# Prompt attention: the order in which ScalarE moves turned probabilities and takes exponentials

## The chip, the cores and the metric

The kernel runs on one core of a Trainium2 chip. The metric is the device time of one execution in microseconds (us). Before the change three runs took 2003.85, 2005.93 and 2006.01 us, with a median of 2005.93 us. Durations below come from one more execution, taken with the hardware profiler.

Five engines work side by side, each through its own instruction list in order: TensorE (PE; its weight loads are the rows "PEld"), VectorE (DVE), ScalarE (ACT), GpSimd (POOL) and SyncE (SP). They meet only at semaphores.

## The reference, cut to what matters

The program is one inference step of a decoder layer for a prompt of 512 tokens and 8 sample sequences of 8 tokens. The change touches only the prompt's sparse attention. There 8 query heads share 2 key/value heads, and each query attends in three branches, each with its own softmax: 31 compressed keys, selected blocks, and a sliding window. With 512 prompt tokens the selected blocks and the window both come to every earlier key.

```python
scale = NSA_HD ** -0.5
s_c = jnp.einsum('qhgd,nhd->qhgn', q, kc) * scale
p_c = masked_softmax(s_c, m_c, -1)
o_c = jnp.einsum('qhgn,nhd->qhgd', p_c, vc.astype(jnp.float32))
...
s_s = jnp.einsum('qhgd,qhnld->qhgnl', q, k_sel) * scale
p_s = masked_softmax(s_s, m_s, (-2, -1))
o_s = jnp.einsum('qhgnl,qhnld->qhgd', p_s, v_sel.astype(jnp.float32))
s_w = jnp.einsum('qhgd,khd->qhgk', q, win_k) * scale
p_w = masked_softmax(s_w, m_w, -1)
o_w = jnp.einsum('qhgk,khd->qhgd', p_w, win_v.astype(jnp.float32))
return gates[..., 0:1] * o_c + gates[..., 1:2] * o_s + gates[..., 2:3] * o_w
```

The softmax is exp(s - max) divided by its sum; the kernel takes the maximum on VectorE, the exponential with its sum on ScalarE, and the division as a factor on the output.

## The kernel before

The program is a row of stages (`project`, `gla`, `compress`, `prompt_attention`, `sample_attention`, `output_and_router`, `experts`, `combine`). All engines meet in a barrier after each stage, so a stage starts when the slowest engine has ended the one before it.

`prompt_attention` (L1053) works through 16 units, u = 0 to 15. A unit is one tile of 128 queries (tile t = u // 4) and one head of each of the two key/value groups (g = u % 4). It uses (t+1) x 128 keys, so that units 0 to 3 have 128 keys, 4 to 7 have 256, 8 to 11 have 384, and 12 to 15 have 512. For each unit:

- TensorE computes the scores: `score_cmp(u)` (L1267, L1268) for the compressed keys, `scores(u, 0)` and `scores(u, 1)` (L1279, L1284) for the selected and the window branch.
- VectorE takes the maxima: `max_cmp(u)` (L1201) and `maxima(u, b)` (L1209), each ended by the small operation of `negated` (L1194).
- ScalarE takes the exponentials: `exp_cmp(u)` (two instructions, L1143) and `exps(u, b)` (two instructions, L1152). In the profile each has a companion row that reads the accumulator.
- TensorE turns the probabilities so that keys lie on partitions: `to_key_major(u, r)` (L1295 for r = 0, L1300 for r = 1 to 4). Here r = 0 is the compressed branch, 1 and 2 are the selected branch's two heads, 3 and 4 the window's. The results go alternately to two PSUM banks, so turn number k waits until turn number k-2 has been moved out.
- ScalarE moves r = 0, 2, 4 out of PSUM and VectorE moves r = 1, 3 (`move`, L1135 on ScalarE, L1111 on VectorE).
- TensorE multiplies by the values, `values(u)` (L1312, L1320), ScalarE copies that result out (`copy_out(u)`, also a row of L1135, 128x384), TensorE turns it back, `back(u)` (L1331), and VectorE weighs and adds (`finish(u)`, first row L1227).

The order of each engine is written out by hand. TensorE's loop body for unit u is: `scores(u+1, 0)`, turns 0 and 1, `score_cmp(u+1)`, turns 2, 3 and 4, `scores(u+1, 1)`, `back(u-1)`, `values(u)`. VectorE's is: `maxima(u, 1)`, `maxima(u+1, 0)`, move 1, `max_cmp(u+1)`, move 3, `finish(u-1)`, `factors(u)`. `back(u-1)` writes to the bank that holds the compressed scores of unit u+1, and so it waits for `exp_cmp(u+1)`:

```python
pe.wait_ge(s_oc, u + 1)
pe.wait_ge(s_pc, min(u + 3, NU))
```

(here u is the unit turned back.)

Of the kernel before, what the change touches and what calls it, by code (L numbers as in the profile page):

```python
# [1052 lines left out]
def prompt_attention(core):  # L1053
# [34 lines left out]
    s_pt, s_pta, s_ptd = (core.sem(n) for n in ("pT_ps", "pT_by_act", "pT_by_dve"))  # L1088
# [3 lines left out]
    def keys_of(u):  # L1092
        return (u // GRP + 1) * P
# [10 lines left out]
    def move(eng, u, r, copy):  # L1104

        k = NR * u + r
        eng.wait_ge(s_pt, k + 1)
        if r == 0:
            return copy(pTc[0:NCMP_P], ps[0:NCMP_P, TURN + k % 2, 0:KVH * P].rearrange("p (h n) -> p h n", h=KVH))
        b, h = divmod(r - 1, KVH)  # L1110
        return copy(pT[:, b, h, 0:keys_of(u)], ps[:, TURN + k % 2, 0:keys_of(u)])  # L1111

    with nc.Block() as block:
        @block.gpsimd
        def _(pool):
            for h in range(KVH):
                rows = slice(64 * (1 - h), 64 * (1 - h) + 64)
                pool.memset(kzc[rows, h * NCMP_P:(h + 1) * NCMP_P], 0.0).then_inc(s_zero, 1)
            pool.wait_ge(core.s_table, 16)
            for b in range(1, HELD, 2):  # L1120
                load_past(core, pool, b, past_numbers(core, pool, b))
# [10 lines left out]
        @block.scalar  # L1132
        def _(act):
            def copy(o, s):
                return act.activation(o, s, ACT.Copy)  # L1135

            act.activation(gates[:, 0:ST, :], proj[:, 0:ST, C_NG:C_NG + 24], ACT.Exp, scale=-1.0)
            act.activation(gates[0:64, ST, :], proj[0:64, ST, C_NG:C_NG + 24], ACT.Exp, scale=-1.0).then_inc(s_ge, 1)

            def exp_cmp(u):  # L1140
                act.wait_ge(s_mc, u + 1)
                for h in range(KVH):
                    last = act.activation(pc[:, u % 2, h, :], ps[:, BACK, CMP + h * NCMP_P:CMP + (h + 1) * NCMP_P], ACT.Exp,  # L1143
                                          scale=SC, bias=mx[:, u % 2, h:h + 1], accum_out=su[:, u % 2, h:h + 1])
                last.then_inc(s_pc, 1)

            def exps(u, b):
                nk = keys_of(u)
                act.wait_ge(s_m[b], u + 1)
                for h in range(KVH):  # L1150
                    i = 2 + 2 * b + h
                    last = act.activation(pp[:, u % 2, b, h, 0:nk], ps[:, 2 * b + h, 0:nk], ACT.Exp, scale=SC,  # L1152
                                          bias=mx[:, u % 2, i:i + 1], accum_out=su[:, u % 2, i:i + 1])
                last.then_inc(s_p[b], 1)

            def copy_out(u):
                act.wait_ge(s_o, u + 1)
                copy(oT, ps[:, OUT, 0:3 * P].rearrange("p (b n) -> p b n", b=3)).then_inc(s_oc, 1)

            exp_cmp(0)  # L1160
            exps(0, 0)
            for u in range(NU):
                exps(u, 1)
                if u >= 1:
                    copy_out(u - 1)
                move(act, u, 0, copy).then_inc(s_pta, 1)
                if u + 1 < NU:
                    exps(u + 1, 0)
                    exp_cmp(u + 1)
                for r in (2, 4):  # L1170
                    move(act, u, r, copy).then_inc(s_pta, 1)
            copy_out(NU - 1)

        @block.vector
# [1506 lines left out]
```

## Time and profile before

| | |
|---|---|
| median of three runs | 2005.93 us |
| the profiled execution's own time | 2008.63 us |
| its span (first to last instruction) | 2006.9 us |
| prompt attention in the span | about 415 to 572 us |
| TensorE / VectorE / ScalarE busy over the span | 88% / 73% / 55% |
| mean granted clock of TensorE over the span | 0.92 of full speed |

A row of the profile's timeline gives the start, the duration, the engine, the source line, the operation, output and input, the count of instructions merged in the row, and in brackets how long the engine stood idle before it and which instruction released it. The share of busy time is a mean over stages that differ; the stage of the change is read by itself.

### The profile page before, as it was taken

To read this page: it belongs to the slowest core of one execution; us is meant where nothing else is said; L and a number is where in the kernel's file an instruction comes from. 1 tells how busy PE (TensorE), PEld (TensorE's weight loads), DVE (VectorE), ACT (ScalarE), POOL (GpSimd) and SP (SyncE) were. 2 spreads that over 40 slices of the span, in tenths; PEclk is the share of its full clock that TensorE was granted. 3 is DMA by queue.
4 is the path that set the end of the run, shared out by engine and by line. 5 is a ranking of instruction groups with operands and counts; after the bars stand their busy time and mean duration, and the time that the engine had idled before them with its cause. 6 is when DMAs were issued, how large, how long until landed. Compare 5 with 4: busy or idle time off the path is not lost. (4 is left out here: it accounts for less than half of the span.)

```text
span 2006.9 us, 27108 instructions
## 1 busy us (share of the span) xinstructions
PE 1774.5 (88%) x8969; PEld 1374.5 (68%) x8969; DVE 1458.5 (73%) x1372; ACT 1103.6 (55%) x1040; POOL 284.4 (14%) x311
## 2 busy tenths in 40 slices
PE   4999757877867795899999999999999999999982
PEld 3777645655545443688888888888888888888872
DVE  4421267344544266889999999999999999999993
ACT  3211233334423131667777777777777777777772
POOL 0000100230001040111212112121211212112110
PEclk9999877967878896899999999999999999999996
DMA  9353351450002713789999999999999999999973
GB/s 357 117 188 121 71 163 47 125 189 1 1 1 65 250 60 148 272 317 371 368 376 365 371 366 369 375 365 375 367 370 374 366 374 373 372 370 363 382 273 115
DMA packets 112070, 516.53 MB, mean 257 GB/s; under 512 B 25853, under 2 KB 47117, under 8 KB 59242
## 3 DMA queue, kind: packets, MB, share of 16 engines
q1 hardware_dynamic: 99098, 485.77, 64.7%
q0 software_dynamic: 12912, 29.98, 5.5%
q8 instruction: 35, 0.57, 0.1%
q14 instruction: 25, 0.20, 0.0%
HBM read 502.69 MB, written 31.81 MB: 266 GB/s over the span
## 5 line engine op out<-in xcount | busy, mean ns | idle before, releaser
L2349 PE MATMUL banks<-split 128*128 128x512 f32 x4608 | 1082.0, 394 | 1.6 <-DVE split L2504 1.6
L2349 PEld LDWEIGHTS banks<-split 128*128 128x128 f32 x4608 | 863.6, 189 | 195.7 <-issue 14.7
L2504 DVE TENSOR_TENSOR split<-expert_buffers,split 128x2048 fp32r<-128x2048 f32 x384 | 867.6, 2286 | 63.1 <-ACT split L2439 61.1
L2439 ACT ACTIVATE split<-expert_buffers 128x2048 fp32r<-128x2048 f32 x384 | 733.3, 1917 | 251.5 <-PE banks L2349 232.7
L2287 POOL TENSOR_TENSOR expert_buffers<-routing 128x1 f32<-128x1 f32 x63 | 61.1, 970 | 912.5 <-PE banks L2356 530.9
L443 PE MATMUL banks<-w_in_high,hT_high 128*128 128x476 f32 (+1 forms) x240 | 93.4, 389 | 7.7 <-DVE hT_low L369 7.7
L443 PE MATMUL banks<-w_in_low,hT_high 128*128 128x476 f32 (+1 forms) x240 | 91.7, 382 | 0.0
L382 DVE COPY arena<-banks 128x476 f32<-128x476 f32 (+1 forms) x15 | 9.8, 651 | 112.3 <-PE banks L443 112.3
L443 PE MATMUL banks<-w_in_high,hT_low 128*128 128x476 f32 (+1 forms) x240 | 91.4, 381 | 0.0
L302 ACT ACTIVATE arena<-banks 128x476 f32<-128x476 f32 (+1 forms) x15 | 8.5, 567 | 126.5 <-PE banks L443 126.5
L2508 DVE TENSOR_TENSOR split<-banks,split 128x1024 fp32r<-128x1024 f32 x64 | 77.8, 1215 | 0.2 <-ACT split L2442 0.2
L1887 PE MATMUL banks<-arena 128*128 128x512 f32 (+1 forms) x160 | 74.3, 624 | 0.6 <-ACT arena L1955 0.6
L1152 ACT ACTIVATE arena<-banks,arena 128x128 f32<-128x128 f32 (+3 forms) x64 | 32.9, 517 | 68.1 <-DVE arena L1194 68.1
L2442 ACT ACTIVATE split<-banks 128x1024 fp32r<-128x1024 f32 x64 | 64.7, 1010 | 9.6 <-PE banks L2356 9.6
L443 PEld LDWEIGHTS banks<-w_in_high,hT_high 128*128 128x128 f32 (+1 forms) x240 | 43.2, 180 | 30.3 <-issue 21.5
L2462 ACT ACTIVATE expert_buffers<-banks,expert_buffers 128x1024 f32<-128x1024 f32 x32 | 35.7, 1117 | 46.3 <-PE banks L2349 46.3
L1300 PE MATMUL banks<-arena 128*128 128x128 f32 x160 | 33.0, 325 | 28.3 <-ACT arena L1135 27.3
L1887 PEld LDWEIGHTS banks<-arena 128*128 128x128 f32 (+1 forms) x160 | 29.7, 189 | 40.3 <-issue 39.5
L2310 POOL DMA_INDIRECT ffn_rows<-expert_buffers x32 | 53.0, 1656 | 5.3 <-issue 5.3
L443 PEld LDWEIGHTS banks<-w_in_high,hT_low 128*128 128x128 f32 (+1 forms) x240 | 43.2, 180 | 9.5
L443 PEld LDWEIGHTS banks<-w_in_low,hT_high 128*128 128x128 f32 (+1 forms) x240 | 43.2, 180 | 8.7
L2454 ACT ACTIVATE expert_buffers<-expert_buffers 128x1024 f32<-128x1024 f32 x32 | 34.0, 1062 | 26.1 <-DVE expert_buffers L2515 26.1
(336 smaller groups left out, 1810.6 us busy)
## 6 DMA issues: line engine op xcount, KB each, us to landing
expert_buffers<-in_w_gate SPq DMA_DIRECT2D x128, 1024.0 KB, 7.6
expert_buffers<-in_w_up SPq DMA_DIRECT2D x128, 1024.0 KB, 7.4
expert_buffers<-in_w_down SPq DMA_DIRECT2D x128, 1024.0 KB, 8.8
arena<-in_w_ada SPq DMA_DIRECT2D x16, 1024.0 KB, 4.8
w_in_landing<-in_w_in SPq DMA_DIRECT2D x6, 1904.0 KB, 15.9
arena<-in_w_ada SPq DMA_DIRECT2D x4, 2048.0 KB, 19.2
arena<-in_x_prompt SPq DMA_DIRECT2D x8, 512.0 KB, 10.1
arena<-in_cache_cmp POOLq DMA_DIRECT2D x32, 128.0 KB, 3.5
```

The lines of the kernel that those rows point to most:

```text
L443: last = pe.matmul(ps[0:n, 4 + (NT * c + t) % 4, 0:CW], h[:, kt, t0:t0 + n].bitcast(F32R), w[:, kt, :].bitcast(F32R), start=(kt == 0 and j ...
L1300: last = pe.transpose(ps[:, TURN + k % 2, kb * P:(kb + 1) * P], pp[:, u % 2, b, h, kb * P:(kb + 1) * P], ident)
L1887: last = pe.matmul(ps[0:n, 4 + 2 * (t % 2) + c, :], mixT[:, kt, t0:t0 + n], wout[:, kt, c * 512:(c + 1) * 512], start=(kt == 0), stop=(kt ...
L2287: pool.tensor_tensor(sums[s_sum.index(sem)], one, one, ALU.add).then_inc(sem, 1)
L2310: pool.indirect_dma_start(core.ffn_d, bass.IndirectOffsetOnAxis(ap=row_out.bitcast(U32), axis=0), y, None, bounds_check=NTOK - 1, oob_is_e ...
L2349: last = pe.matmul(ps[:, bank + c, :], x[:, kt * P:(kt + 1) * P].bitcast(F32R), wt.bitcast(F32R), start=False, stop=(kt == KT - 1 and x is ...
L2439: act.activation(high[:, j % RING_Q].bitcast(F32R), v, ACT.Copy).then_inc(s_high, 1)
L2442: act.activation(dst.bitcast(F32R), ps[:, TB:TB + 2, :].rearrange("p b n -> p (b n)"), ACT.Copy).then_inc(sem, 1)
L2454: act.activation(s, g, ACT.Sigmoid, scale=ALPHA).then_inc(s_sig, 1)
L2462: act.activation(y, ps[:, DB:DB + 2, :].rearrange("p b n -> p (b n)"), ACT.Copy, scale=weight_out).then_inc(s_y, 1)
L2504: dve.tensor_tensor(rest[:, j % RING_Q].bitcast(F32R), v, high[:, j % RING_Q], ALU.subtract).then_inc(s_rest, 1)
L2508: dve.tensor_tensor(lo.bitcast(F32R), ps[:, TB:TB + 2, :].rearrange("p b n -> p (b n)"), hi, ALU.subtract).then_inc(out, 1)
```

## The change

In ScalarE's loop the exponentials of the next unit's selected and compressed branch, which stood between move 0 and move 2 of a unit, are issued after move 4, the compressed one first. The window exponentials are only written at another place of the loop: they still follow and still precede the next unit's `copy_out`.

```diff
             exp_cmp(0)
             exps(0, 0)
+            exps(0, 1)
             for u in range(NU):
-                exps(u, 1)
                 if u >= 1:
                     copy_out(u - 1)
-                move(act, u, 0, copy).then_inc(s_pta, 1)
+                for r in (0, 2, 4):
+                    move(act, u, r, copy).then_inc(s_pta, 1)
                 if u + 1 < NU:
+                    exp_cmp(u + 1)
                     exps(u + 1, 0)
-                    exp_cmp(u + 1)
-                for r in (2, 4):
-                    move(act, u, r, copy).then_inc(s_pta, 1)
+                    exps(u + 1, 1)
             copy_out(NU - 1)
```

The instructions on every other engine keep their order. On ScalarE, in units 13 and 14 (512 keys), these rows stand before the change; L1152 are exponentials, L1143 the compressed exponentials, L1135 with 128x384 is `copy_out`, with 31x256 move 0, with 128x512 moves 2 and 4:

```order
L1152 ACTIVATE arena<-banks,arena 128x512 x2
L1135 ACTIVATE arena<-banks 128x384
L1135 ACTIVATE arena<-banks 31x256
L1152 ACTIVATE arena<-banks,arena 128x512 x2
L1143 ACTIVATE arena<-banks,arena 128x31 x2
L1135 ACTIVATE arena<-banks 128x512 x2
L1152 ACTIVATE arena<-banks,arena 128x512 x2
L1135 ACTIVATE arena<-banks 128x384
L1135 ACTIVATE arena<-banks 31x256
```

and these stand there after it:

```order
L1152 ACTIVATE arena<-banks,arena 128x512 x4
L1135 ACTIVATE arena<-banks 128x384
L1135 ACTIVATE arena<-banks 31x256
L1135 ACTIVATE arena<-banks 128x512 x2
L1143 ACTIVATE arena<-banks,arena 128x31 x2
L1152 ACTIVATE arena<-banks,arena 128x512 x4
L1135 ACTIVATE arena<-banks 128x384
```

Between move 0 and move 2 four exponentials have gone; they now stand behind move 4, where the window's two follow them directly.

On ScalarE at the start of the stage (units 0 and 1, 128 keys) the difference is:

```order
 L1152 ACTIVATE arena<-banks,arena 128x128 x4
 L1135 ACTIVATE arena<-banks 31x256
-L1152 ACTIVATE arena<-banks,arena 128x128 x2
-L1143 ACTIVATE arena<-banks,arena 128x31 x2
 L1135 ACTIVATE arena<-banks 128x128 x2
-L1152 ACTIVATE arena<-banks,arena 128x128 x2
-L1135 ACTIVATE arena<-banks 128x384
-L1135 ACTIVATE arena<-banks 31x256
-L1152 ACTIVATE arena<-banks,arena 128x128 x2
-L1143 ACTIVATE arena<-banks,arena 128x31 x2
+L1143 ACTIVATE arena<-banks,arena 128x31 x2
+L1152 ACTIVATE arena<-banks,arena 128x128 x4
```

The four exponentials of unit 0 alone before the loop are the same; from move 0 on the same exchange is made in each of the units 0 to 14.

## Rows read from the trace of the kernel before

**Rows 1.** The page's head.
```profile
span 2006.9 us, 27108 instructions
```

**Rows 2.** Stretches, TensorE alone: length, PE busy (instructions), granted clock, DMA share, GB/s.
```profile
core 0: us, PE busy (x), PEclk, DMA share, GB/s
415.00:450.00 35.00, 30.56 (x185) 0.50 0.83 271
450.00:571.00 121.00, 95.63 (x744) 0.81 0.00 1
573.00:650.00 77.00, 56.74 (x436) 0.82 0.14 43
```

**Rows 3.** Waits from 415 to 572 us: total us, times, longest.
```profile
ACT arena L1152 <- DVE arena L1194: 68.1, 20, 5.9
DVE arena L1227 <- PE banks L1331: 49.1, 16, 4.7
PE banks L1300 <- ACT arena L1135: 27.3, 25, 2.5
```

**Rows 4.** Timeline of unit 14 (512 keys), from turn 2 to `back`.
```profile
552.32 1.09 PE L1300 MATMUL banks<-arena 128*128 128x128 f32 x8 [1.10 <-ACT arena L1135]
...
553.50 0.26 ACT L1143 ACTIVATE arena<-banks,arena 128x31 f32<-128x31 f32 x1
...
553.93 0.19 ACT L1143 ACTIVATION_READ_ACCUMULATOR arena<-banks,arena 128x1 f32 x1
554.02 0.57 ACT L1135 ACTIVATE arena<-banks 128x512 f32<-128x512 f32 x1
...
554.65 0.65 PE L1300 MATMUL banks<-arena 128*128 128x128 f32 x4 [1.24 <-ACT arena L1135]
...
555.34 0.60 ACT L1135 ACTIVATE arena<-banks 128x512 f32<-128x512 f32 x1 [0.74 <-PE banks L1300]
...
556.40 0.55 PE L1331 MATMUL banks<-arena 128*128 128x128 f32 x3
```

**Rows 5.** Timeline of unit 15, the last: turns 2 and 3, turn 4's weights.
```profile
562.45 2.46 PE L1300 MATMUL banks<-arena 128*128 128x128 f32 x12 [2.47 <-ACT arena L1135]
...
563.79 0.71 PEld L1300 LDWEIGHTS banks<-arena 128*128 128x128 f32 x4 [0.44 <-ACT arena L1135]
```

**Rows 6.** Timeline of unit 2 (128 keys), from turn 2 to `back`.
```profile
434.77 0.69 PE L1300 MATMUL banks<-arena 128*128 128x128 f32 x2 [0.35 <-ACT arena L1135]
...
435.83 0.25 ACT L1135 ACTIVATE arena<-banks 128x128 f32<-128x128 f32 x1
436.13 0.48 PE L1300 MATMUL banks<-arena 128*128 128x128 f32 x1 [0.68 <-ACT arena L1135]
...
436.65 0.28 ACT L1135 ACTIVATE arena<-banks 128x128 f32<-128x128 f32 x1 [0.56 <-PE banks L1300]
...
437.49 0.90 PE L1331 MATMUL banks<-arena 128*128 128x128 f32 x3
```

**Rows 7.** Timeline of unit 6 (256 keys), from turn 2 to `back`.
```profile
468.16 0.66 PE L1300 MATMUL banks<-arena 128*128 128x128 f32 x4 [1.66 <-ACT arena L1135]
...
469.44 0.36 ACT L1135 ACTIVATE arena<-banks 128x256 f32<-128x256 f32 x1
...
469.85 0.44 PE L1300 MATMUL banks<-arena 128*128 128x128 f32 x2 [1.03 <-ACT arena L1135]
...
470.32 0.38 ACT L1135 ACTIVATE arena<-banks 128x256 f32<-128x256 f32 x1 [0.53 <-PE banks L1300]
...
470.96 0.86 PE L1331 MATMUL banks<-arena 128*128 128x128 f32 x3
```

**Rows 8.** Timeline of unit 12: its selected exponentials for unit 13 wait for VectorE.
```profile
530.41 0.69 ACT L1152 ACTIVATE arena<-banks,arena 128x512 f32<-128x512 f32 x1 [0.66 <-DVE arena L1194]
```

**Rows 9.** Timeline of unit 13, at the lower clock: turn 4 and `back`.
```profile
543.07 1.11 PE L1300 MATMUL banks<-arena 128*128 128x128 f32 x4 [1.23 <-ACT arena L1135]
...
546.27 0.55 PE L1331 MATMUL banks<-arena 128*128 128x128 f32 x3
```

## The prediction, made before the changed kernel had run

> **What bounds the kernel now.** I read four views, in this order. The page's head gives the span, 2006.9 us [rows 1]. The stretches show where the change lies: 415 to 572 us, an eighth of the span, where TensorE is busy but not full (95.6 of 121 us from 450 on) and the DMA share is 0.00 from 450 to 571 [rows 2]. No transfer sets anything there, and none runs through the stage's end that a shorter stage would have to wait for. As all engines meet in a barrier behind the stage, what it saves should reach the end of the kernel one for one.
>
> The waits show that no engine bounds the stage by its work; a ring of waits does. ScalarE waits for a maximum of VectorE (68.1 us), VectorE waits for `back` (49.1 us), and TensorE waits for a move of ScalarE before its turns (27.3 us in 25 waits) [rows 3]. The code closes the ring. The window exponentials of unit u+1 need VectorE's maximum, which stands behind `finish(u-1)`, which needs `back(u-1)`, which stands on TensorE behind turn 4 of unit u, which needs move 2 of unit u. So whatever brings move 2 forward brings the whole next unit forward. The timeline then shows the link that the change touches: in unit 14 turns 2 and 3 start at 552.32, ScalarE in that time takes the exponentials of unit 15, move 2 comes at 554.02 and turn 4 at 554.65, after a pause of 1.24 us [rows 4].
>
> **The change, part by part.** It removes no instruction and adds none. In units 0 to 14, four exponentials leave the place between move 0 and move 2 and go behind move 4. No DMA and no queue of SP or POOL is passed.
>
> *First term, the way from turn 2 to turn 4.* Before, it is 554.65 - 552.32 = 2.33 us with 512 keys [rows 4], 1.69 with 256 keys [rows 7], 1.36 with 128 keys [rows 6]. After, ScalarE stands free at move 2, so the way is: start of a turn to start of its move, then start of move 2 to start of turn 4. Both pieces are in the rows, since move 4 already waits for its turn alone. With 512 keys they are 0.69 and 0.63, together 1.32 [rows 4]; with 256 keys 0.47 and 0.41, together 0.88 [rows 7]; with 128 keys 0.52 and 0.30, together 0.82 [rows 6]. The last unit has no next unit, so it already runs in the new order, and there it took 563.79 - 562.45 = 1.34 us [rows 5]. I take that as the measured proof of 1.32. Turn 3 also has to be over before turn 4; turns 2 and 3 together last 1.09 us at 512 keys [rows 4], so they fit below 1.32 unless turn 3 has to wait for VectorE's move 1.
>
> The gain for one unit is 0.54 (128 keys), 0.81 (256) and 0.99 (512). For 384 keys I set 0.90, an estimate halfway between its neighbours. The sum is 4 x 0.54 + 4 x 0.81 + 4 x 0.90 + 3 x 0.99 = 12.0 us. In three units the moved exponentials had themselves been waiting for VectorE before move 2; the longest of these waits is 0.66 us [rows 8], so they bring between 0.7 and 2.0 us more. I take 1.4. First term: -13.4 us. Its bounds: zero, if something else holds turn 4; and, if the pause before turn 4 closed entirely, 0.68, 1.03 and 1.24 us a unit [rows 6, 7, 4] with 1.14 for 384 keys, together 15.1 us.
>
> *Second term, a new wait in `back`.* `back(u-1)` needs `exp_cmp(u+1)`, since both use one PSUM bank. That was long done; now it is queued behind move 4. Counted from the start of turn 4, it ends after the start of move 4, that move's length, and 0.62 us for the two small exponentials (553.50 to 554.12 [rows 4]). With 512 keys this is 0.69 + 0.60 + 0.62 = 1.91, and `back` starts at 1.75: late by 0.16 us [rows 4]. With 256 keys it is 0.47 + 0.38 + 0.62 = 1.47 against 1.11: late by 0.36 [rows 7]. With 128 keys 1.42 against 1.36: late by 0.06 [rows 6]. Where TensorE runs at the lower clock its scores last longer and cover it: unit 13 has 3.20 us in that place [rows 9]. The mean clock of 0.81 [rows 2] means that (1 - 0.81) / 0.5 = 38% of the time from 450 us on is spent at the lower clock, 62% at the higher. With 0.26 for 384 keys: 3 x 0.06 + 0.62 x (4 x 0.36 + 4 x 0.26 + 3 x 0.16) = 2.0 us. Bounds: 0, and 14 x 0.36 = 5.0. I take +2.0, from the middle, since both clocks occur in every tile. Behind the waiting `back` TensorE has only `values(u)`; VectorE's `finish` waits for it, and that is the ring.
>
> *Third term, what else moves.* The selected exponentials of unit u+1 now end at about 1.91 + 2 x 0.69 = 3.3 us behind the start of turn 4 (0.69 is one of them [rows 8]). Their takers are TensorE's `scores(u+2, 0)` and turn 1 of the next unit, both behind `back` (1.75) and a whole `values(u)`; unit 14 has `values` still to come at 556.40, and the exponentials would end at about 557.9. The cover is `values(u)`; without it the price would be some 1 us a unit. ScalarE's own slack before the window exponentials is 68.1 us in 20 waits, 3.4 us each [rows 3], and the moved work takes 1.8 us of it. VectorE keeps its order. I set this term at 0, between 0 and +1 us.
>
> Sum: -13.4 + 2.0 = -11.4 us. The profiled execution took 2008.63 us, 2.7 above the median of the runs; by its own time the changed kernel would take 1997.2, and taken from the median 2005.93 it is **1994.5 us**. The clock is assumed to be spent as before.
>
> **The clock.** In this stage the granted clock is 0.50 until 450 us and has a mean of 0.81 after it [rows 2]; the two levels are 1.2 and 2.4 GHz. In the trace it falls while TensorE does a unit with two pauses close together, as in unit 13, where the pause before turn 4 is 1.23 us and everything behind it is at the lower level [rows 9]. The change shortens the second pause of each pair. This works for me or not at all, as far as the pauses decide. The lower level makes 3.20 out of 1.75 us from turn 4 to `back` [rows 4, 9], 1.45 us a unit.
>
> The Trainium skill, TensorE: Matmul & The Clock Gate, has two sections that pull apart here. "HAM oscillation" lays the fall to waits for DMA that are longer than any pause in these rows; by it the clock would not answer to this change, and the sum stays at -11.4. "A second HAM failure mode" lets short pauses between groups of matmuls do it; by it the second rival below would be likely. The trace speaks for the second, since the clock falls here with pauses of 1.2 us, but no run yet shows that shortening them helps.
>
> **Rivals.**
>
> *The clock stays up.* Fewer or shorter pauses keep TensorE at the higher level. Of the 11 units from 450 us on, 38% are 4.2 units; at 1.45 us each that is 6.1 us more: 1988.4, with 1984 to 1991 around it if the first units rise earlier too. For it: the falls come behind the pauses. Against it: the other pause, before turn 2 (1.10 us in unit 14 [rows 4]), stays as long as it was.
>
> *The compressed exponentials cost more.* If the higher clock holds, the new wait in `back` is paid by every unit, and late moves of VectorE hold turn 3 in some. With 5.0 for the second term and a first term of 11, the gain is 6: 1999.9, with 1997.5 to 2001.9 around it. For it: at 256 keys 0.36 us is almost half of the gain. Against it: it needs all units at its worst price.
>
> *The change doesn't do what it says.* Turn 4 turns out to be held by something that starts no earlier (turn 3, or VectorE's move 1), or the clock takes back what the order gives. Then the time is 2002 to 2009. Against it: unit 15 did the same way in 1.34 us.
>
> *Slower than before.* One mechanism: a denser pattern that the gate answers with the lower clock in the units that now run high, and that continues into the sample attention behind it. The other 62% of 11 units are 6.8, at 1.45 us 9.9 us, which brings the time to 2004.4. Sample attention takes 77 us with a mean of 0.82 [rows 2], so 64% at the higher level, 49 us; a quarter of that stretched by 3.20 / 1.75 costs 10 us, on the path where TensorE is busy (56.7 of 77 us), 7.5: 2011.9. It decides from the point at which the clock costs more than 11.4 us. Against it: TensorE is busier after the change, not less.
>
> **How the numbers follow.** Two-tenths of a per cent, 4 us, is about what a measurement of this kernel can tell from no change. The chances: forecast (1991 to 1997.5) 0.52; clock stays up 0.22; compressed exponentials 0.13; no change 0.09; slower 0.04. Faster by over 0.2% (under 2001.9) holds the first three, 0.87; within it 0.09; slower 0.04. The range for 8 in 10 takes most of the second case and most of the third: 1986 to 2000.5.
>
> **What would show it.** Right: in the changed profile turn 2 to turn 4 takes about 1.3 us with 512 keys and 0.9 with 256; ScalarE's move 2 shows a wait for a turn of TensorE in each unit, not only in unit 15; the stage ends about 11 us earlier and the stages behind it keep their lengths; `back` names ScalarE's L1143 as its releaser in units at the higher clock, for 0.1 to 0.4 us. Wrong: turn 4 waiting for VectorE's L1111; TensorE's `scores(u+2, 0)` waiting for L1152; a mean clock from 450 us to the stage's end far from 0.81; or a stage shorter by 11 us with a kernel that is not.

## The result and the profile after

The changed kernel took 1986.07 us (median of four runs, 1984.04 to 1995.06) against 2005.97 us; the ratio is 0.9903 with a 95% interval of 0.9881 to 0.9926. In six more runs it took 1987.63 us, ratio 0.9901 (0.9882 to 0.9919). So it is 18 to 20 us faster. The first median lies inside the stated range of 1986.0 to 2000.5 by 0.07 us, and 8 us below the forecast of 1994.5.

The profiled execution of after took 1995.06 us, the slowest of its runs, with a span of 1993.4. Three views of it answer to rows of before. First the stretches of the stage (length, PE busy, granted clock, DMA share, GB/s), which answer to [rows 2]:

```profile
core 0: us, PE busy (x), PEclk, DMA share, GB/s
414.50:450.00 35.50, 28.88 (x205) 0.69 0.81 267
450.00:553.00 103.00, 85.75 (x729) 0.87 0.01 1
```

The stage ends at 553 instead of 571 us, and the clock is higher in both stretches: 0.69 against 0.50, 0.87 against 0.81. (In the second profiles, shown below, only the later stretch is higher.) With the same instructions TensorE is busy for 114.6 us instead of 126.2.

Then the waits from 415 to 562 us, which answer to [rows 3]:

```profile
ACT arena L1152 <- DVE arena L1194: 43.1, 17, 3.9
DVE arena L1227 <- PE banks L1331: 33.5, 16, 3.4
...
ACT arena L1135 <- PE banks L1300: 22.0, 32, 1.2
PE banks L1300 <- ACT arena L1135: 20.5, 23, 2.5
...
PE banks L1331 <- ACT arena L1143: 0.5, 1, 0.5
```

All links of the ring wait less (68.1 to 43.1, 49.1 to 33.5), and ScalarE's moves now wait 32 times for a turn. The last row is the new wait of `back` for the compressed exponentials; the view names it in one unit only, and in the others it shows no pause before `back` or puts it down to "issue".

Then unit 14, which answers to [rows 4]:

```profile
536.91 1.09 PE L1300 MATMUL banks<-arena 128*128 128x128 f32 x8 [1.10 <-ACT arena L1135]
...
537.60 0.60 ACT L1135 ACTIVATE arena<-banks 128x512 f32<-128x512 f32 x1 [0.74 <-PE banks L1300]
...
538.25 0.66 PE L1300 MATMUL banks<-arena 128*128 128x128 f32 x4 [0.25 <-ACT arena L1135]
...
538.95 0.60 ACT L1135 ACTIVATE arena<-banks 128x512 f32<-128x512 f32 x1 [0.75 <-PE banks L1300]
...
539.44 0.28 ACT L1143 ACTIVATE arena<-banks,arena 128x31 f32<-128x31 f32 x1
...
539.87 0.21 ACT L1143 ACTIVATION_READ_ACCUMULATOR arena<-banks,arena 128x1 f32 x1
...
540.18 0.52 PE L1331 MATMUL banks<-arena 128*128 128x128 f32 x3
```

Turn 2 to turn 4 takes 538.25 - 536.91 = 1.34 us, where it took 2.33. `back` comes 1.93 us behind turn 4, right behind the accumulator read that ends at 540.08, where it came after 1.75.

To see where the stage's time went I cut it into five pieces by the starts of three instructions of each unit: VectorE's move 3 (L1111), ScalarE's move 4 (L1135) and VectorE's `finish` (L1227). The pieces are summed over the units (worked out from the timelines; the first reaches from the stage's first matmul to move 3 of unit 1, the last is the distance of the last two `finish`; each figure is good to 0.1 us). The runs behind the second profiles and the other kernels are told below.

| us | start | `finish` to move 3 | move 3 to move 4 | move 4 to `finish` | last | stage |
|---|---|---|---|---|---|---|
| before | 12.7 | 85.0 | 25.0 | 28.0 | 5.4 | 156.1 |
| before, second profile | 12.7 | 87.4 | 24.8 | 27.8 | 4.3 | 157.0 |
| after | 12.3 | 83.6 | 11.3 | 28.1 | 3.5 | 138.8 |
| after, second profile | 12.2 | 82.3 | 11.3 | 25.6 | 3.5 | 134.9 |
| compressed ones between moves 2 and 4 | 12.2 | 83.3 | 10.8 | 24.8 | 4.7 | 135.8 |
| only the compressed ones moved | 12.2 | 83.2 | 15.5 | 27.2 | 3.5 | 141.6 |
| only the selected ones moved | 12.6 | 81.4 | 15.1 | 24.9 | 3.5 | 137.5 |
| before with filled pauses | 12.7 | 82.8 | 23.5 | 26.3 | 3.5 | 148.7 |
| `copy_out` early | 12.2 | 79.0 | 10.7 | 24.0 | 3.5 | 129.3 |
| the same with filled pauses | 12.7 | 75.7 | 11.5 | 20.2 | 3.5 | 123.5 |

The piece from move 3 to move 4 holds what was reordered, and it fell by 13.7 us in both profiles of after. The rest of the gain lies in the other pieces: 3.6 us in one and 7.5 us in the other against the first profile of before, 4.7 and 8.6 against the second. No instruction of the ring changed its place in them. One, from move 4 to `finish`, even holds the new wait of `back`.

The first profile's span fell by 13.5 us although its stage fell by 17.3. Output and router, far behind the stage and untouched, took 147.8 us instead of 144.9 there, and 144.7 us in the second profile of after. Between the starts of the loads of `w_out` and of the first expert product, the profiles of all kernels here scatter from 144.7 to 150.5 us, whatever was changed. So a single profile of the whole kernel is good to some 5 us at best, and the stage is read by itself. On the mean of two profiles each the stage gained 19.7 us, and the medians of the whole kernel 18 to 20, so the gain did pass the barrier nearly one for one.

### The profile page after: what moved, and what is told of

Same layout as the page of the kernel before. It is cut to its first block and busy times, and to the rows that moved or that the text cites. A ratio compares the mean times of both kernels' runs of the same rounds, so it can differ in the third digit from the quotient of the medians.

```text
span 1993.4 us, 27108 instructions
## 1 busy us (share of the span) xinstructions
PE 1764.6 (89%) x8969; PEld 1368.1 (69%) x8969; DVE 1458.6 (73%) x1372; ACT 1105.0 (55%) x1040; POOL 285.0 (14%) x311
## 5 line engine op out<-in xcount | busy, mean ns | idle before, releaser
L443 PEld LDWEIGHTS banks<-w_in_high,hT_high 128*128 128x128 f32 (+1 forms) x240 | 43.1, 180 | 30.3 <-issue 21.5
L1152 ACT ACTIVATE arena<-banks,arena 128x128 f32<-128x128 f32 (+3 forms) x64 | 33.3, 531 | 43.1 <-DVE arena L1194 43.1
L1300 PE MATMUL banks<-arena 128*128 128x128 f32 x160 | 32.0, 322 | 21.0 <-ACT arena L1135 20.5
## 6 DMA issues: line engine op xcount, KB each, us to landing
w_in_landing<-in_w_in SPq DMA_DIRECT2D x6, 1904.0 KB, 15.9
```

The source lines that it names most:

```text
L443: last = pe.matmul(ps[0:n, 4 + (NT * c + t) % 4, 0:CW], h[:, kt, t0:t0 + n].bitcast(F32R), w[:, kt, :].bitcast(F32R), start=(kt == 0 and j ...
```

## The experiments

Times are medians; ratios are against the kernel before on the same chip, which took 2005.86 us beside four of these kernels (after again, the compressed ones alone, the compressed ones between the moves, before with filled pauses) and 2006.43 us beside the other four. Where an edit adds lines, the line numbers of what follows are a few higher: the turns L1300 are L1301 to L1305 there, and `back`, L1331, is L1332 to L1336. The edits are shown against the kernel after, where nothing else is said.

**The kernel after and the kernel before once more.**

> The changed kernel once more, unchanged, to see how far its time scatters and where the scatter lies. Path theory (the order on the ring gives 11.4 us, the rest of the 19.9 is the clock): the prompt stage again lasts about 139 us from its first score to its last finish (156.1 before, 138.8 in the first profile of after), turn 2 to turn 4 again takes 1.34 us at 512 keys, and what differs between runs lies in the stages behind it. Rival (the stage itself scatters by 5 us or more with the clock): the stage lasts 133 to 146 us and the scatter of the total follows it. Total 1984 to 1990.

> The kernel before once more, unchanged, for a second profile of its prompt stage. If its stage is a steady 156 us (first profile: 156.1, mean clock 0.74), the 17 to 21 us between it and the two profiles of after are the change's own. If the clock scatters in it too, it lasts 150 to 158 us with a mean clock of 0.74 to 0.80, and part of the distance to after is chance. The way from turn 3 to move 4, summed over units 1 to 15, should be 25.0 us again in either case, within 1 us.

After took 1987.63 us (1983.6 to 1989.97). The kernel before took 2005.69 us, ratio 0.9995 (0.9977 to 1.0013). The stage of before is steady: 156.1 and 157.0 us. That of after is 138.8 and 134.9, and here the first theory was too strict, since the stage scatters by 4 us. The stretches of the second profile of after and of before:

```profile
414.00:450.00 36.00, 33.85 (x199) 0.50 0.79 264
450.00:549.00 99.00, 80.10 (x731) 0.93 0.00 1
```

```profile
412.00:450.00 38.00, 30.36 (x205) 0.63 0.77 250
450.00:569.00 119.00, 95.76 (x727) 0.78 0.00 1
```

From 450 us on, before has 0.81 and 0.78, after 0.87 and 0.93. Until 450 us there is no such order: 0.50 and 0.63 against 0.69 and 0.50. Over the whole stage it is 0.74 and 0.75 against 0.82 and 0.82, so the higher clock is no accident of one profile. The two profiles of after have the same mean and still differ by 3.9 us, so the mean alone does not give the time; they differ in where the lower clock lies, early or late in the stage.

**Each half of the change alone.** Only the compressed exponentials go behind move 4:

```diff
-                for r in (0, 2, 4):
+                move(act, u, 0, copy).then_inc(s_pta, 1)
+                if u + 1 < NU:
+                    exps(u + 1, 0)
+                for r in (2, 4):
                     move(act, u, r, copy).then_inc(s_pta, 1)
                 if u + 1 < NU:
                     exp_cmp(u + 1)
-                    exps(u + 1, 0)
                     exps(u + 1, 1)
```

> Half of the change: the selected exponentials of the next unit stay between move 0 and move 2 as before, and only the compressed ones go behind move 4. Path theory: turn 2 to turn 4 shortens by the 0.52 us of these two instructions in each of 15 units, -7.8 us, and back pays the new wait, +2; so -5.8 us against before, 2000. If the clock follows the pause before turn 4 (here 0.7 instead of 1.2 us), 2 to 5 us more: 1995 to 1998. If only the whole pause matters to the clock, 2000. If the gain came from the selected exponentials alone: 2006 or above.

It took 1995.47 us, ratio 0.9933 (0.9911 to 0.9956). In a unit of 512 keys the timeline reads:

```profile
539.12 1.09 PE L1302 MATMUL banks<-arena 128*128 128x128 f32 x8 [1.10 <-ACT arena L1135]
...
540.92 0.66 PE L1302 MATMUL banks<-arena 128*128 128x128 f32 x4 [0.71 <-ACT arena L1135]
```

Turn 2 to turn 4 is 1.80 us, 0.53 less than the 2.33 of [rows 4], as the path theory has it. Summed over the units move 3 to move 4 fell by 9.5 us, more than the 7.8 expected; the kernel fell by 10.4, and the clock of the stage rose from 0.74 to 0.80. That is the expectation with a clock that answers.

Only the selected exponentials go behind move 4:

```diff
-                for r in (0, 2, 4):
+                move(act, u, 0, copy).then_inc(s_pta, 1)
+                if u + 1 < NU:
+                    exp_cmp(u + 1)
+                for r in (2, 4):
                     move(act, u, r, copy).then_inc(s_pta, 1)
                 if u + 1 < NU:
-                    exp_cmp(u + 1)
                     exps(u + 1, 0)
                     exps(u + 1, 1)
```

> The other half of the change: only the selected exponentials go behind move 4; the compressed ones stay between move 0 and move 2. Path theory: ScalarE is idle between move 0 and move 2 of after for 0.42 us (128 keys) to 0.75 us (512 keys), and the compressed exponentials take 0.52, so move 2 is late by at most 0.1 us in the smaller units; and back does not wait for them. The kernel is within 1.5 us of after, 1986 to 1989. If the order gains strictly by what is taken away in front of move 2 (no cover by the turn itself), it is 7.8 us slower than after: 1995. Together with the run that moved the compressed ones alone (-10.4 us) it says whether the two halves add up.

It took 1993.3 us, ratio 0.9927 (0.9905 to 0.9949), which reaches from 1987 to 1996 us, so the kernel's time refutes neither expectation. The pieces refute both: against after, move 3 to move 4 is neither unchanged nor 7.8 us longer, but 3.8 us longer. I had the cover of 0.52 us right and overlooked what these exponentials wait for. The timeline of an early unit:

```profile
425.90 0.29 ACT L1143 ACTIVATE arena<-banks,arena 128x31 f32<-128x31 f32 x1 [0.67 <-DVE arena L1196]
...
426.44 0.27 ACT L1135 ACTIVATE arena<-banks 128x128 f32<-128x128 f32 x1
426.76 0.18 PEld L1302 LDWEIGHTS banks<-arena 128*128 128x128 f32 x1 [1.17 <-ACT arena L1135]
```

VectorE gives the compressed maximum only behind its move 1, so ScalarE stands before L1143 and move 2 stands behind it. Before, the selected exponentials covered that: in this stage ScalarE waited for VectorE before L1143 once, 3.2 us at the stage's start, and here it waits 11 times, 7.7 us in all. Move 3 to move 4 is 15.1 us, 3.8 more than in after.

The halves gained 10.4 and 13.1 us, together 23.5, more than the 18 to 20 of both together; the intervals of these times are too wide to build on that, but the piece from move 3 to move 4 shows the same, 9.5 and 9.9 against 13.7. In a unit of 512 keys the halves take 0.53 and 0.78 us out of the way from turn 2 to turn 4, and both together only 0.99, because then ScalarE waits 0.74 us for turn 2 itself. What fits into that wait costs nothing, so the second half has less left to gain.

**The new wait of `back` taken away.** The compressed exponentials go between move 2 and move 4:

```diff
-                for r in (0, 2, 4):
+                for r in (0, 2):
                     move(act, u, r, copy).then_inc(s_pta, 1)
                 if u + 1 < NU:
                     exp_cmp(u + 1)
+                move(act, u, 4, copy).then_inc(s_pta, 1)
+                if u + 1 < NU:
                     exps(u + 1, 0)
                     exps(u + 1, 1)
```

> As after, but the compressed exponentials of the next unit are issued between move 2 and move 4 instead of behind move 4. In after ScalarE stands idle there for 0.42 to 1.0 us in every unit, and these exponentials take 0.52 to 0.62. Theory (the new wait of back for them is real and costs 0.1 to 0.5 us in units at the higher clock): back no longer names L1143, and the kernel is 2 us faster than after (1 to 3). Rival (back would wait as long for something else): same as after within 1 us. Second rival (0.52 does not fit into the gap at 128 keys and delays move 4): slower than after by up to 1 us.

The timeline of a unit of 512 keys:

```profile
532.26 0.66 PE L1302 MATMUL banks<-arena 128*128 128x128 f32 x4 [0.25 <-ACT arena L1135]
...
532.36 0.29 ACT L1143 ACTIVATE arena<-banks,arena 128x31 f32<-128x31 f32 x1
...
532.95 0.60 ACT L1135 ACTIVATE arena<-banks 128x512 f32<-128x512 f32 x1 [0.21 <-PE banks L1302]
...
534.01 0.55 PE L1333 MATMUL banks<-arena 128*128 128x128 f32 x3
```

Here `back` starts 534.01 - 532.26 = 1.75 us behind turn 4, exactly the distance of before, so the wait is real and is gone. Yet the kernel took 1988.07 us (ratio 0.9909, 0.9889 to 0.9929), the same as after. The piece from move 4 to `finish` is 24.8 us, where the two profiles of after have 25.6 and 28.1; those two are of one and the same kernel, so the difference from 24.8 is no measure of the wait. The expected 2 us did not show in the time, whose interval is 4 us wide on each side, so the runs can neither confirm nor exclude them.

**The pauses of the kernel before filled.** TensorE gets 6, 8 or 10 small matmuls between turn 3 and turn 4; their results are not used. The edit is shown against the kernel before:

```diff
+            def fill(n):
+                for _ in range(n):
+                    pe.matmul(ps[:, OUT, 3 * P:4 * P], identb, identb, start=True, stop=True)
...
                 for r in range(NR):
+                    if r == 4:
+                        fill((6, 8, 10, 10)[u // GRP])
                     to_key_major(u, r)
```

> The kernel before with 6 (128 keys), 8 (256) or 10 (384, 512) additional matmuls of bf16 128x128 per unit in the pause between turn 3 and turn 4, into PSUM columns that nothing reads. They compute nothing that is used. They take about 0.1 us each at the lower clock and less at the higher, so they fit into pauses of 0.68, 1.03 and 1.24 us. Clock theory (the granted clock falls behind these pauses, and the change gained some 6 us by shortening them): the mean clock from 450 us to the stage's end rises from 0.81 towards 0.9 or more, and the kernel is 4 to 10 us faster than before with its order unchanged. Rival (the clock has nothing to do with these pauses): same as before within 1 us, or up to 3 us slower where the additional matmuls run over the pause.

It took 1999.31 us (1996.26 to 2006.14), ratio 0.9966 (0.9950 to 0.9981): 6.5 us faster with more work and the order unchanged. The stage and one of its units:

```profile
413.00:450.00 37.00, 32.80 (x227) 0.59 0.78 257
450.00:562.00 112.00, 93.03 (x837) 0.87 0.00 1
```

```profile
545.73 1.09 PE L1304 MATMUL banks<-arena 128*128 128x128 f32 x8 [1.09 <-ACT arena L1135]
546.66 0.72 PE L1290 MATMUL banks<-arena 128*128 128x128 bf16 x10
...
548.05 0.66 PE L1304 MATMUL banks<-arena 128*128 128x128 f32 x4 [0.67 <-ACT arena L1135]
```

Turn 2 to turn 4 is 2.32 us as before, so the path did not get shorter; the clock from 450 us on is 0.87 instead of 0.81 and 0.78, and the stage lasts 148.7 instead of 156.1 and 157.0. So work put in this pause held the clock up in this stage, and the higher clock was worth some 7 us. This does not show whether the pause's length or TensorE's total work decides, nor whether it matters that the added work is ordinary matmuls between transposes.

**Further along the ring.** `copy_out` of a unit goes in front of the next window exponentials, where ScalarE stands idle anyway. The edit is shown against the kernel with the compressed ones between moves 2 and 4:

```diff
             for u in range(NU):
-                if u >= 1:
-                    copy_out(u - 1)
...
                 if u + 1 < NU:
                     exps(u + 1, 0)
+                copy_out(u)
+                if u + 1 < NU:
                     exps(u + 1, 1)
-            copy_out(NU - 1)
```

> The compressed exponentials between move 2 and move 4, and copy_out of a unit in front of the next unit's window exponentials instead of behind them. ScalarE stands idle there for 2.5 to 3.9 us before these exponentials, and copy_out takes 0.37 to 0.49, which now lies on the ring between the exponentials and move 0. Theory (the ring is what counts): 0.37 us in each of up to 15 units, less where values(u) ends late (256 keys), so 4 to 5.5 us faster than after: 1982 to 1984. Rival (copy_out now waits for values(u) and holds up the window exponentials): same as after or up to 3 us slower. Clock rival: the ring gets shorter as said, but the clock takes 2 us or more of it back.

It took 1978.15 us (1976.71 to 1981.85), ratio 0.9859 (0.9835 to 0.9883). By the ratios that is 8 to 9 us faster than after and 10 us faster than the kernel it is built on (0.9909), more than the 4 to 5.5 expected. Its timeline at 512 keys:

```profile
523.65 0.49 ACT L1135 ACTIVATE arena<-banks 128x384 f32<-128x384 f32 x1 [1.98 <-PE banks L1321]
...
524.71 0.69 ACT L1152 ACTIVATE arena<-banks,arena 128x512 f32<-128x512 f32 x1 [0.57 <-DVE arena L1195]
...
526.06 0.36 ACT L1135 ACTIVATE arena<-banks 31x256 f32<-31x256 f32 x1
...
526.47 1.09 PE L1301 MATMUL banks<-arena 128*128 128x128 f32 x8 [0.72 <-ACT arena L1135]
```

In unit 14 of before the window exponentials started here:

```profile
550.20 0.69 ACT L1152 ACTIVATE arena<-banks,arena 128x512 f32<-128x512 f32 x1 [5.38 <-DVE arena L1194]
```

With `copy_out` early they still wait for VectorE, not for `copy_out`, and turn 2 starts 526.47 - 524.71 = 1.76 us behind them; before, it was 552.32 - 550.20 = 2.12 [rows 4]. The difference is 0.36 us a unit, as expected. The stage is 129.3 us, 6.5 under the kernel it is built on and 5.6 to 9.5 under the two profiles of after; what goes beyond 15 x 0.36 = 5.4 us is within the scatter of 3.9 us that after itself shows.

The same order with six small matmuls (`fill` as above), results unused, in the longest pause, before turn 2, shown against the kernel with `copy_out` early:

```diff
                     if r == 1 and u + 1 < NU:
                         score_cmp(u + 1)
+                        if u >= 1:
+                            pe.wait_ge(s_oc, u)
+                            fill(6)
```

> As the run with copy_out early, plus 6 additional bf16 matmuls 128x128 per unit in TensorE's longest pause, between the compressed scores and turn 2 (1.0 to 1.9 us in after), into columns that nothing reads. They compute nothing that is used. Clock theory: the granted clock of the stage rises from about 0.82 to 0.9 or more and the kernel is 3 to 8 us faster than the one without them, 1976 to 1980. Rival (the clock answers to something else than the pauses): same within 1 us, or slower by up to 0.3 us a unit where the additional matmuls run into turn 2.

It took 1975.28 us (1971.84 to 1978.5), ratio 0.9838 (0.9815 to 0.9862), the fastest of all, just beyond the expected 1976 to 1980. The stage's mean clock is 0.92 instead of 0.81 and the stage 123.5 instead of 129.3 us:

```profile
412.60:450.00 37.40, 31.88 (x273) 0.77 0.78 254
450.00:536.00 86.00, 74.43 (x739) 0.98 0.01 2
```

Of these 5.8 us the whole kernel shows 2.9, with intervals that overlap, so on the kernel's time this last step is not settled; the profile of this run has the longest output and router part of all, 150.5 us.

## Why the prediction was right, and where its size was off

*The bound.* Right. A ring of waits bounds the stage; bringing move 2 forward shortened all of it, and the gain passed the barrier.

*First term, -13.4 us.* Right in kind and size. Turn 2 to turn 4 came to 1.34 us at 512 keys (1.32 worked out), and move 3 to move 4 fell by 13.7 us, within the bounds of 0 and 15.1. Measured as the term was worked out, from turn 2 to turn 4 and summed over units 0 to 14, it fell from 29.7 and 30.5 us in the two profiles of before to 16.1 and 15.9 us. Unit 15 of before [rows 5] was a fair sample of the new order. The term needed both halves: with the selected ones alone it was 9.9, with the compressed ones alone 9.5.

*Second term, +2.0 us.* The mechanism was right, and so were its pieces at the higher clock: from move 4 to `finish` 1.79 us in after against 1.65 in before at 512 keys (0.14; 0.16 worked out), 1.58 against 1.22 at 256 keys (0.36, as worked out), and both 1.65 and 1.22 again with the wait taken away. In the last unit of a tile it costs less than I had, 0.14 in unit 7 and 0.03 in unit 11, since the scores that stand before `back` there are those of the next, longer unit. Added up over units 4 to 14 at the higher clock, the pieces come to 2.4 us, so 2.0 is a fair size for the delay. That the kernel would be 2 us faster without it is not shown: its time was the same.

*Third term, 0.* Right as far as the rows show: `scores(u+2, 0)` does not wait for the moved exponentials in after; its one wait for L1152 is the 0.8 us of unit 0's start, the same as before.

*"The clock is assumed to be spent as before".* This is the step that failed, and the gap of 8 us is mostly it. From 450 us on the clock rose from 0.81 and 0.78 to 0.87 and 0.93. The order's part, 13.7 less some 2, is close to the 11.4 of the sum; the stage gained 17.3 to 22.1 us, and what is left is 5.6 to 10.4 us for which the sum had nothing. The measured time lies where the rival *The clock stays up* (1988.4, 1984 to 1991) had it, to which I gave a chance of 0.22; the prediction also calls it "the second rival", though it stands first in the list. So the time left the band of the forecast, 1991 to 1997.5. That 1986.07 lies inside the range of 1986 to 2000.5 is luck: the margin is 0.07 us, and the first four runs of after spread over 11 us. A mean clock far from 0.81, which I had named as a sign of being wrong, is what came. The reason that I gave against that rival, that the pause before turn 2 stays as long, did not hold: it does stay (1.10 us before and after), and the clock rose all the same. The run with filled pauses shows that work in the one pause is enough, 6.5 us with nothing else changed. In the prediction I priced this at 6.1 us and then left it out of the sum, with the trace's own falls behind pauses already pointing to it.

The falls that are left in after from 447 us on all come within 2 us of the pause before turn 2, where it lasts 1.4 to 2.5 us. Two things that I read there were too simple. In unit 13 not everything behind turn 4 is at the lower level: the clock was low from 542.7 to 546.1 us, and `back` takes 0.55 us as in [rows 4]. And a pair of pauses does not always bring the clock down: unit 14 of before has 1.10 and 1.24 us, and its turn 4 and scores still ran at the higher level.

Of the two sections of the Trainium skill's page TensorE: Matmul & The Clock Gate, "A second HAM failure mode" is the one that these runs bear out; by "HAM oscillation" alone before and its filled version would have had the same clock, and they had 0.74 and 0.80 over the stage.

*The signs.* Turn 2 to turn 4 took 1.34 us at 512 keys and with 256 keys 0.92 and 0.91 in two of the four units, but 1.16 and 1.14 in the other two; move 2 waited for a turn in all 16 units, as I had said. `back` was to name L1143 in the units at the higher clock; it does so in one unit, and the wait is shown by its distance from turn 4 and by its going away with the other order, not by the name.

*The other rivals.* The compressed exponentials as a large cost are refuted by the time and by the 2.4 us above. That the change doesn't do what it says is refuted by the 1.34 us. The lower clock in a denser pattern did not come about in the stage of any of the six reordered kernels. The sample attention behind it took 89.3 and 89.2 us after and 88.6 before.

Not settled: what of the clock's part comes from the length of the pause and what from TensorE's busy share; whether the kernel of the new order gains anything by losing the wait of `back`; and why output and router scatter by 5 us.

## What to carry to other kernels

Where a ring of short waits bounds a stage, look for the instruction on the ring that has work standing in front of it which nobody on the ring needs yet, and move that work into a wait that the same engine already has; the last unit of a loop often shows the new distance before the change is built. Before moving work into a wait, read what it waits for itself: the compressed exponentials fitted by length between move 0 and move 2 and still cost 3.8 us, since their maximum came late. And where a trace shows the clock falling behind pauses that a change shortens, put the clock's price into the sum.

## What the hardware showed that I had not expected

Work whose results nobody reads made a kernel faster: six to ten matmuls of bf16 128x128 a unit, some 0.07 us each at the higher clock (10 in 0.72 us), brought 6.5 us at an unchanged order and an unchanged 2.32 us from turn 2 to turn 4. With six a unit in the longest pause the mean granted clock of the stage reached 0.92, against 0.74 and 0.75 in before.
